# Modulation blocks summed beside projections, and narrow experts placed between wide ones

## What is computed

```python
# first block: layer 0 = even mixer, cross attention, dense swiglu (2816 hidden)
#              layer 1 = conformer convolution, cross attention, mixture of 8 experts (3584 hidden, top 2)
h = h + even_mixer(rmsnorm(h), ...);      h = h + cross_attn(rmsnorm(h), mem, ...)
h = h + swiglu(rmsnorm(h), w_gu, w_down)
h = h + conformer_conv(rmsnorm(h), ...);  h = h + cross_attn(rmsnorm(h), mem, ...)
h = h + moe_swiglu(rmsnorm(h), router, w_gu, w_down)
# second block: its layers are modulated by a vector c
cs = silu(c)
for l in range(2):
    mod = cs @ ada_w[l] + ada_b[l]        # 1024 x 6144 weights per layer
    sh1, sc1, g1, sh2, sc2, g2 = split(mod, 6)
    x = x + g1 * mixer_l(rms_norm(x, norm1_g[l]) * (1 + sc1) + sh1)
    x = x + g2 * hier_moe(rms_norm(x, norm2_g[l]) * (1 + sc2) + sh2, ...)   # 16 experts, 256 hidden
```

## Time and profile before

| | us |
|---|---|
| median of 3 runs | 2881.32 |
| lowest and highest | 2875.06, 2892.28 |
| the profiled execution, whole | 2874.71 |
| its span | 2872.9 |
| first mixture, first gather to last scatter | 985.5 |
| second block, first mixture, norm to norm | 225.9 |
| second block, second mixture, norm to norm | 212.6 |
| PE busy in the span | 2539.0 (88%) |
| DVE, ACT busy in the span | 794.5 (28%), 410.5 (14%) |

### The profile page before, as it was taken

One profiled execution on the slowest core, in us unless ns is written; L12 is line 12 of the kernel. 1 busy time (PEld: TensorE's weight loads), 2 busy tenths in 40 slices (PEclk: granted clock), 3 DMA queues, 4 the chain that ended last, 5 costly groups with the idle time before them and its releaser, 6 DMA issues. The chain is left out here.

```text
span 2872.9 us, 35384 instructions
## 1 busy us (share of the span) xinstructions
PE 2539.0 (88%) x15219; PEld 1502.3 (52%) x15219; DVE 794.5 (28%) x1806; ACT 410.5 (14%) x926; POOL 53.7 (2%) x67
## 2 busy tenths in 40 slices
PE   2889899998989999999997878689689977998997
PEld 2776788785773333333333323265554466656543
DVE  1211221288221122221212000124434413373122
ACT  1102000001121111011110000113211101352111
POOL 0000000070000000000000000000000000000000
PEclk9999999998989999999999999898879988697899
DMA  8333255642009999999999999932139962301481
GB/s 268 117 109 126 73 191 205 209 143 74 1 31 392 393 385 385 379 373 393 371 393 393 393 394 393 391 108 88 53 120 371 374 122 80 117 1 63 159 300 56
DMA packets 328586, 645.33 MB, mean 225 GB/s; under 512 B 12875, under 2 KB 98017, under 8 KB 328417
## 3 DMA queue, kind: packets, MB, share of 16 engines
q1 hardware_dynamic: 318608, 636.51, 61.4%
q10 hardware_dynamic: 9809, 6.41, 0.8%
HBM read 641.84 MB, written 1.05 MB: 224 GB/s over the span
## 5 line engine op out<-in xcount | busy, mean ns | idle before, releaser
L1330 PE MATMUL bank<-ring,xn 128*32 128x512 f32 x4896 | 564.3, 596 | 7.9 <-DMA ring<-od_moe_gu 6.2
L1142 PE MATMUL bank<-xn,ring 128*128 128x256 f32 x2048 | 462.9, 390 | 54.2 <-DVE xn L2878 17.7
L1142 PEld LDWEIGHTS bank<-xn,ring 128*128 128x128 f32 x2048 | 401.1, 196 | 116.6 <-issue 41.1
L1330 PEld LDWEIGHTS bank<-ring,xn 128*32 128x32 f32 x4896 | 157.1, 110 | 362.3 <-issue 349.0
L1395 PE MATMUL bank<-ring,att 128*32 128x512 f32 x2448 | 276.7, 593 | 1.3 <-ACT att L1961 1.3
L1295 PE MATMUL bank<-ring,xn 128*64 128x512 f32 x336 | 170.8, 658 | 64.9 <-issue 64.9
L2406 DVE TENSOR_TENSOR sq<-att,bank 32x512 f32<-32x512 f32 x70 | 48.0, 686 | 507.8 <-ACT att L1972 342.4
L1297 PE MATMUL bank<-ring,xn 128*64 128x512 f32 x336 | 171.2, 659 | 0.0
L1395 PEld LDWEIGHTS bank<-ring,att 128*32 128x32 f32 x2448 | 78.6, 110 | 171.9 <-issue 170.8
L1249 PE MATMUL bank<-xn,ring 128*128 128x256 f32 x704 | 153.6, 380 | 0.0
L1249 PEld LDWEIGHTS bank<-xn,ring 128*128 128x128 f32 x704 | 134.6, 191 | 18.7 <-issue 0.3
(11 more groups left out here) (265 smaller groups left out, 2324.0 us busy)
## 6 DMA issues: line engine op xcount, KB each, us to landing
ring<-od_moe_gu SPq DMA_DIRECT2D x112, 2048.0 KB, 17.3
ring<-od_moe_down SPq DMA_DIRECT2D x56, 2048.0 KB, 18.0
ring<-ada_w SPq DMA_DIRECT2D x24, 2048.0 KB, 15.1
ring<-moe_w_gate SPq DMA_DIRECT2D x32, 1024.0 KB, 9.2
ring<-moe_w_up SPq DMA_DIRECT2D x32, 1024.0 KB, 8.4
ring<-moe_w_down SPq DMA_DIRECT2D x16, 2048.0 KB, 13.8
ring<-ev_w_in SPq DMA_DIRECT2D x10, 2048.0 KB, 19.8
ring<-ev_ffn_gu SPq DMA_DIRECT2D x10, 2048.0 KB, 12.8
```

Of the source, the lines that this page charges most:

```text
L1142: mm = nc.tensor.matmul(ps[:, c * T:(c + 1) * T], kblk(b)[:, k, u * T + c * P:u * T + (c + 1) * P], x[:, k, :], start=k == 0, stop=k == KD ...
L1330: return nc.tensor.matmul(PSB[f.b][j * QP:(j + 1) * QP, :], src[:, k, at:at + QP], kblk(b)[:, k, :], start=k == 0, stop=k == KD - 1)
```

## The change

Three things. First, `linear` and `token_linear` take a function `beside`, and a turn of the modulation work stands beside a unit of a projection: its block in the ring behind the projection's block, its DVE sum in DVE's queue at that unit, and the PE sum of the turn before behind the unit. 3 blocks go beside the output projection of the even mixer, 9 beside keys, values and queries of the first cross attention, 5 stay in the dense stage, 4 go beside the queries of the second cross attention and 3 beside its output. That is all 24. The calls in the mixtures stay, but find nothing left. Outside the dense stage the partial sums lie in `att` in place of `sq`. Second, the scales that combine `mod` with the norms' gains are made before the norm of the first mixture, and no longer inside later stages. Third, the experts of the first mixture run in the order `TURNS` of the sorted loads: widths 96, 96, 64, 96, 64, 96, 96, 64. `st.i` is now the turn and `st.rank` the place in the sort.

```diff
+TURNS = [0, 1, 5, 2, 6, 3, 4, 7]
...
+        def ada_acc(a):
+
+            home = sq.rearrange("p k t -> p (k t)") if a.in_sq else att
+            return home[:, a.i % 2 * WBLK:(a.i % 2 + 1) * WBLK]
...
+        def ada_block(in_sq=True):
...
+            if ada_made[0] == 2 * ADA_BLOCKS:
+                return None
+            a = Stage()
+            a.i, a.in_sq = ada_made[0], in_sq
+            a.block = block(col_load(A["ada_w_2"][a.i // ADA_BLOCKS], a.i % ADA_BLOCKS * WBLK))
...
+            a.block.release = (ada_ready, a.n + 1)
+            ada_made[0] += 1
+            return a
...
+        def ada_turns(n):
+
+            left = [n]
+
+            def beside():
+                x = Stage()
+                made = left[0] > 0
+                left[0] -= made
+                ada_turn(x, ada_block(False) if made else None)
+                return x
+            return beside
+
+        def linear(W, c0, n, done, beside=None):
...
+            st.units, st.beside = [], []
             st.done = counted(done)
             for at in range(c0, c0 + n, WBLK):
                 b = block(col_load(W, at))
                 for u in range(2):
                     st.units.append((b, u, fill_turn((done, count(done, 1) + 1))))
+                    st.beside.append(beside() if beside is not None else None)
...
-        ev_out = linear(A["ev_w_out"][0], 0, D, h_ready)
+        ev_out = linear(A["ev_w_out"][0], 0, D, h_ready, ada_turns(3))
...
-            st.k = linear(A["xa_wkv"][l], 0, D, proj_ready)
-            st.v = token_linear(A["xa_wkv"][l], D, D, proj_ready)
+            st.k = linear(A["xa_wkv"][l], 0, D, proj_ready, beside)
+            st.v = token_linear(A["xa_wkv"][l], D, D, proj_ready, beside)
...
-            st.kv = memory_kv(l) if kv is None else kv
-            st.q = linear(A["xa_wq"][l], 0, D, proj_ready)
+            st.kv = memory_kv(l, beside) if kv is None else kv
+            st.q = linear(A["xa_wq"][l], 0, D, proj_ready, beside)
...
-            st.out = linear(A["xa_wo"][l], 0, D, h_ready)
+            st.out = linear(A["xa_wo"][l], 0, D, h_ready, beside_out)
...
-        cross0 = cross(0, ev_out.end, None)
+        cross0 = cross(0, ev_out.end, None, ada_turns(9))
...
-        cross1 = cross(1, pw2.end, kv1)
+        cross1 = cross(1, pw2.end, kv1, ada_turns(4), ada_turns(3))
...
-        for i, cap in enumerate(CAPS):
+        for n, i in enumerate(TURNS):
+            cap = CAPS[i]
...
-            st.i, st.width, st.gather, st.blocks = i, cap, gather_fills, (first_block, len(blocks))
+            st.i, st.rank, st.width, st.gather, st.blocks = n, i, cap, gather_fills, (first_block, len(blocks))
...
-                expert = sp.value_load(order[0:1, st.i:st.i + 1], min_val=0, max_val=E1 - 1)
+                expert = sp.value_load(order[0:1, st.rank:st.rank + 1], min_val=0, max_val=E1 - 1)
...
+            def sums_beside(st, i):
+                if st.beside[i] is not None:
+                    ada_sums(st.beside[i].ada)
+
             def pe_linear(st, x, ready):
                 for i, (b, u, f) in enumerate(st.units):
                     if u == 0:
                         landed(b)
                     unit(b, u, f, x, ready if i == 0 else None)
+                    sums_beside(st, i)
...
-                for b, c, f in st.units:
+                for i, (b, c, f) in enumerate(st.units):
                     if c == 0:
                         landed(b)
                     token_unit(b, c, f, x)
+                    sums_beside(st, i)
...
+            def steps_beside(st):
+                for x in st.beside:
+                    if x is not None:
+                        ada_step(x)
+
             def add_units(st):
 
                 for i, (b, u, f) in enumerate(st.units):
+                    if st.beside[i] is not None:
+                        ada_step(st.beside[i])
                     hp = h[:, 2 * i:2 * i + 2, :]
                     nc.vector.tensor_tensor(hp, full(f).rearrange("p (c t) -> p c t", c=2), hp, ALU.add)\
...
                     norm_memory(st.l)
+                    steps_beside(st.kv.k)
+                    steps_beside(st.kv.v)
+                steps_beside(st.q)
                 dve_attention(st.att)
                 add_units(st.out)
...
-                if l == 0:
-                    ada_scales(1)
...
+            dve.wait_ge(scalar_step, 1)
             add_units(ev_out)
             dve_cross(cross0, True)
             normalise(norm_ffn, vec("ev_norm_ffn"))
-            dve.wait_ge(scalar_step, 1)
...
+            ada_scales(0)
+            ada_scales(1)
             normalise(norm_moe, vec("od_norm_moe"))
...
-                    weigh_slots(st.i, P, "pairs").then_inc(scatter_ready, 1)
+                    weigh_slots(st.rank, P, "pairs").then_inc(scatter_ready, 1)
...
-                    take_slots(st.i + 1, CAPS[st.i + 1]).then_inc(gather_ready, 1)
+                    after_it = moe1[st.i + 1]
+                    take_slots(after_it.rank, after_it.width).then_inc(gather_ready, 1)
...
-            ada_scales(0)
```

More of the change, by code:

```diff
@@ L461, in row_load, with ada_turn @@
             return lambda b: (rblk(b)[:, to // P:(to + n) // P, :], src)
-        def linear(W, c0, n, done):
+        ADA_BLOCKS = 6 * D // WBLK
+        ada_made, ada_left = [0], []
+        def ada_block(in_sq=True):
[4 more added lines that the diff above has]
+            a.block = block(col_load(A["ada_w_2"][a.i // ADA_BLOCKS], a.i % ADA_BLOCKS * WBLK))
+            a.n = count(ada_ready, 1)
+            a.block.release = (ada_ready, a.n + 1)
+            ada_made[0] += 1
+            return a
+        def ada_turn(x, a):
+            x.ada, x.ada_in = list(ada_left), [a] if a else []
+            for given in x.ada:
+                given.fill = fill_turn()
+            ada_left[:] = x.ada_in
+        def ada_turns(n):
[8 more added lines that the diff above has]
+        def linear(W, c0, n, done, beside=None):
             st = Stage()
-            st.units = []
+            st.units, st.beside = [], []
             st.done = counted(done)
@@ L476, in linear, with token_linear @@
             return st
-        def token_linear(W, c0, n, done):
+        def token_linear(W, c0, n, done, beside=None):
             st = Stage()
-            st.units = []
+            st.units, st.beside = [], []
             st.done = counted(done)
@@ L502, in stacked_blocks_kernel @@
         chunks = []
[L503 to L523, removed]
         def ffn_steps(n_hidden, gate_up, down, ada_at=(), after_first=None):
@@ L674, in attention, with memory_kv @@
             return st
-        def memory_kv(l):
+        def memory_kv(l, beside=None):
             st = Stage()
@@ L679, in memory_kv, with cross @@
             st.memn = count(memn_ready, KD)
-            st.k = linear(A["xa_wkv"][l], 0, D, proj_ready)
-            st.v = token_linear(A["xa_wkv"][l], D, D, proj_ready)
+            st.k = linear(A["xa_wkv"][l], 0, D, proj_ready, beside)
+            st.v = token_linear(A["xa_wkv"][l], D, D, proj_ready, beside)
             return st
-        def cross(l, h_at, kv):
+        def cross(l, h_at, kv, beside, beside_out=None):
             st = Stage()
@@ L730, in stacked_blocks_kernel @@
             b.release = (bank_full[fs[1].b], fs[1].n)
-        pw1.sg = counted(sg_ready) - KD
+        pw1.sg, pw1.beside = counted(sg_ready) - KD, [None] * KD
         kv1 = memory_kv(1)
@@ L738, in stacked_blocks_kernel @@
         pw2 = linear(A["od_pw2_w"][0], 0, D, h_ready)
-        cross1 = cross(1, pw2.end, kv1)
+        cross1 = cross(1, pw2.end, kv1, ada_turns(4), ada_turns(3))
+        assert ada_made[0] == 2 * ADA_BLOCKS and not ada_left
         norm_moe = norm(cross1.out.end)
@@ L788, in stacked_blocks_kernel @@
                 st.before = prev.steps[-1].used
-            gather_fills = four_fills(gathered) if i + 1 < E1 else None
+            gather_fills = four_fills(gathered) if n + 1 < E1 else None
             moe1.append(st)
@@ L1465, in ada_sums @@
                     for j in range(WBLK // P):
-                        mm = nc.tensor.matmul(ps[:, j:j + 1], ada_acc(a.i)[:, j * P:(j + 1) * P], ones[:, 0:1],
+                        mm = nc.tensor.matmul(ps[:, j:j + 1], ada_acc(a)[:, j * P:(j + 1) * P], ones[:, 0:1],
                                               start=True, stop=True)
@@ L2466, in ada_sum @@
                     dve.wait_ge(slot_landed[a.block.slot], a.block.landed)
-                    w, y = kblk(a.block), ada_acc(a.i)
+                    w, y = kblk(a.block), ada_acc(a)
                     chain(nc.vector.tensor_scalar(y, w[:, 0, :], cs[:, 0:1], None, ALU.mult))
@@ L2827, in next_slots @@
                 if st.paired:
-                    weigh_slots(st.i, P, "pairs").then_inc(scatter_ready, 1)
+                    weigh_slots(st.rank, P, "pairs").then_inc(scatter_ready, 1)
                 else:
                     for to, which in zip(scatter_more, ("three0", "three1", "pairs")):
```

(5 more changed lines are left out.)

2 lines of the change are left out of this document (removed).

## The result

| | before | after |
|---|---|---|
| median, us | 2883.04 | 2861.81 |
| lowest and highest, 14 runs each | 2875.06, 2898.47 | 2856.27, 2879.16 |
| the profiled execution, whole | 2874.71 | 2872.88 |
| its span | 2872.9 | 2871.1 |

The ratio is 0.9926, with a 95% interval of 0.9902 to 0.9950: the change makes the kernel faster by 21 us, between 14 and 28 by the interval. The forecast was 46 us less; 2861.8 lies in its range, near the upper end. The profiled execution of after, though, is only 1.8 us shorter than that of before. So there are two questions: why the stages gave less than forecast, and where the profiled execution lost what they gave.

What follows compares the result with a forecast made beforehand. In the first mixture PE bounds wide experts and the weight stream narrow ones. Gains of 55.9 (first mixture) and 13.3 (second mixtures) less 22.8 (projections) make 46 us: 2881.3 - 46 = 2835 us, range 2810 to 2866.

Steps and rivals of the forecast that it cites:

- The lead of the narrow experts: First mixture: weights loaded ahead during wide experts shorten the narrow ones to 102, 102 and 111.2 us.
- The price of seven modulation blocks: Second block's first mixture: without them it matches its twin, 212.62 us in place of 225.90, 13.3 us gained.
- The wide experts: First mixture: PE sets the pace; without modulation sums they take 118, 125.3, 122.9, 122.9 and 125.3 us.
- the count of landings: Narrow expert behind a wide one: block arrivals counted slot by slot, up 6 landing at 89 us, 102 in all.
- Rival (a): First mixture: the ring gives no usable lead, narrow experts stay at 111.9, 111.9 and 121.7 us; 2865 us, chance 0.12.
- (b): First mixture: the lead is worth more and the mixture falls to the stream's time, 905 us; 2810 us, chance 0.08.
- The lower bound of the prediction: Second block's first mixture: PE's own sums for seven modulation blocks, 7 x 0.98 = 6.9 us gained at least.
- What the projections pay: Mixer's output and both attentions: the nineteen modulation blocks moved there cost 22.8 us.
- my two bounds: Projections: PE's sums for one modulation block cost between 0.81 and 0.98 us; 0.98 was taken.
- Rival (c): Projections: DVE's step does not fit beside a unit, each of 19 blocks costs 6.4 us more; 2957 us, chance 0.04.
- The late softmax: Second attention: DVE starts on the scores behind the fourth modulation block's sums, 4.6 us later.
- Rival (d): First mixture: the weight stream sags to 357 GB/s and the mixture gains nothing; 2891 us, chance 0.01.

Runs made afterwards that it cites:

- c2: The changed kernel with a weight ring of 6 slots in place of 7; 2908.85 us, ratio 1.0087.
- c1: The kernel before with the new order of the experts and nothing else; 2878.81 us, ratio 0.997.
- b3: The changed kernel with one modulation block moved from the second attention's queries to the first attention; 2866.6 us, ratio 0.9907.
- a3: The kernel before with sixteen dummy products put ahead of the last layer's compression; 2893.64 us, ratio 1.0005.
- a4: The changed kernel with the experts of the first mixture back in their old order; 2879.77 us, ratio 0.9945.
- b1: The kernel before with the operands of the compression's products exchanged; 2874.69 us, ratio 0.9949.
- b2: The changed kernel with the operands of the compression's products exchanged; 2844.96 us, ratio 0.9849.
- a1: The changed kernel run and profiled once more, nothing edited; 2862.19 us, ratio 0.9893.
- a2: The changed kernel with sixteen dummy products put ahead of the last layer's compression; 2861.55 us, ratio 0.9889.
- b4: The changed kernel with the compression's operands exchanged and one modulation block moved from the second attention's queries to the first; 2838.75 us, ratio 0.9834.

## Why the prediction was right or wrong

Three terms failed. The lead of the narrow experts was counted too large (102, 102 and 111.2 us; measured 108.5, 109.6 and 114.4). The price of seven modulation blocks in the second block's first mixture was set at 13.3 us and measured 7.0. And the clock of the last layer's compression was put at nothing: no term, only the 6.6 us between one execution and the median. Two smaller misses went the other way.

**The wide experts: right, and a little better.** Forecast 118, 125.3, 122.9, 122.9 and 125.3 us; measured 115.7, 125.0, 121.4, 121.4 and 125.0, together 5.9 us less. A wide expert behind a narrow one is 3.6 us shorter and not the 2.4 that I read from the earlier trace rows. The shorter scatter (3.3 us at 1247.74 in place of 5.4) is 2.1 of it; the rest is the last down product of the expert before, which also falls behind the gather (from start to next start 3.6 us for a narrow one, 5.2 for a wide one). The first expert lost all of its waiting but 1.2 us.

**The narrow experts: the mechanism right, the size wrong.** Forecast 102, 102 and 111.2; measured 108.5, 109.6 and 114.4, together 17.2 more. The step that failed is the count of landings. It put gate 3 into the slot of down 0 at 30.5 and landed up 3 at 41 and up 4 at 57. The rows have gate 3 issued at 32.6, step 3 begin at 46.1 and step 4 at 63.5, 6.5 late. From step 4 to the next gather it is 45 us, as counted (57 to 102); all of the miss is ahead of it.

The first 2.1 us are a wrong reading of the earlier trace rows. The count gave the narrow expert a scatter of 3.0 us ("the scatter to 19.4"), but the one that stands in it belongs to the expert before, a wide one, and takes 5.4: from 1140.91 to step 1 at 1146.29, and as much in before (1517.42 to 1522.86). I had used that rule for the wide experts and not for the narrow ones.

The other 4.4 us are the stream. The five blocks from gate 3 to up 4 take 31.0 us from issue to use where I allowed 5 x 5.32 = 26.6, a figure read from a stream that never pauses. Here it had stopped, and it moved only 35 GB/s in the first 1.95 us behind the issue. In the 29.0 us behind them it moved 393 GB/s, 11.4 MB, where five blocks are 10.5: part of the next block had come in before up 4 was whole. So the rows put about 2 us on the restart and about 2 on blocks that overlap; no run isolates either. That the lead in the ring is the source of the gain is shown by c2 and c1. Rival (a) is out, since the narrow experts behind a wide one did become shorter; so is (b).

**The first mixture** gave 44.6 us of the 55.9: 5.9 better and 17.2 worse.

**The second block's first mixture: wrong.** I took the whole difference of 13.3 us between it and its twin as the price of the modulation blocks. It gave 5.6 from norm to norm and 7.0 up to the next projection. Timeline of PE at its end in after, and the end of the twin in after:

```profile
2271.63 2.90 PE L1199 MATMUL bank<-sq,ones 128*128 128x256 f32 x6 [7.20 <-issue]
2278.23 4.11 PE L1199 MATMUL bank<-sq,ones 128*128 128x256 f32 x10 [3.71 <-issue]
...
2851.52 3.69 PE L1199 MATMUL bank<-sq,ones 128*128 128x256 f32 x16 [0.18 <-issue]
```

An idle time of 10.9 us at the norm belongs to the place and not to the blocks: it is there with them (5.12 and 5.58 us in before) and without, and the twin has 0.18. The 7.2 us of it that fall inside the window are nearly all of the 7.7 by which the stage still exceeds its twin. What fills them stays open: the squares that PE sums there were ready in `sq` at 2266.0, and the bracket names no engine. The lower bound of the prediction, 6.9 us for PE's own part, was close to the truth. Two stages that run the same code are not twins where their surroundings differ.

**What the projections pay: right.** Forecast 22.8 us, measured 18.7. A row of each kind in after:

```profile
153.96 0.95 PE L1490 MATMUL bank<-ones,att 128*128 128x1 f32 x8
154.77 7.15 PE L1160 MATMUL bank<-xn,ring 128*128 128x256 f32 x32
```

Units start 7.8 us apart, without a wait of PE for DVE; a sum pushes the next unit by 0.81 us, the lower of my two bounds (19 x 0.17 = 3.2 us of the difference). Rival (c) is out. The late softmax was counted as 4.6 us and measured by b3 as 4.1; its second price, the fallen clock, was not counted: of the 7.5 us, 4.1 are the wait and 0.8 the fourth block's sum, and 2.6 are left for it. Against before it costs less, since before runs part of this attention at half clock too: from the first transpose to the output projection it is 12.2 us in before, 13.0 in after and 10.5 in b3.

**The sum up to the last layer** was therefore 33 us and not 46.

**The clock: a term that was missing.** I made the sum against one execution, added the 6.6 us between it and the median, and so took for granted that the changed kernel would draw the same clock. The compression's clock differs between executions of one program. Nine traces have the products of 60 columns: the first piece ran at full clock in six of them (not in after, a3 and a4), the second in one alone, that of before. So the execution that the sum was made against was the exception, with full clock in both pieces, and that of after had neither. The medians are medians over such draws: they differ by 21 us in the first comparison and by 34 in the second (2896.5 and 2862.2). With the draw removed (b1, b2) it is 29.7. So 13 us of the miss are in the stages. The 12 between 33 and 21 I put down to the clock; that is argued from the pairs and not measured by itself, since single traces cannot give the share of each draw in a median. A hint stood in the times shown: three runs from 2875 to 2892, 17 us apart.

On the clock the Trainium skill (page "TensorE: Matmul & The Clock Gate", section "Why this matters for your kernels") tells to avoid drops by leaving no idle gap between bursts of products. The trace agrees in the attention of after, where the products behind a wait run at half clock (3.62 us for 1.89). It does not in the compression: the second piece of a1 ran at 0.53 with PE busy for 26.15 of 26.15 us, behind one at 0.98. That every load of the mixture would be held to about 358 GB/s (page "DMA: Bandwidth & Descriptors", section "Bandwidth") is not what the rows of after show: 393 and 394 GB/s over 116 and 121 us. The same section has more for a core that streams alone and keeps that figure for two at once, and with that the rows agree: one core runs here. Rival (d) is out.

## What to carry to other kernels

Work that is moved out of a stage bound by a stream gives back its own time and also the lead that the stream then builds, but only as much of it as the buffers hold, and only if stages with a need for it stand behind ones with time to spare: the two parts were worth 8.2 us more together than singly. Count a stream that has run empty by its own rows, not by the rate of one that never pauses. Ask of each piece of work in a stage whose it is: here the scatter and the last down product belong to the stage before. Do not price a removed step by the difference of two stages with different neighbours. Before a few per cent are judged, look for a stage whose time differs between executions of one kernel, and take that difference out of both kernels; here exchanging the operands of one product was worth 21 us in the kernel before and 17 in the changed one.

## What the runs showed of the hardware

PE's granted clock fell to half inside a stretch of products of 60 columns with weights of 128 x 128, with PE busy all the time, in some executions and not in others of the same program (14.4 to 15.2 us a piece against 25.9 to 27.6). The second of the two pieces was at half clock in eight of nine traces, the first in three. A first piece at full clock, and in a2 sixteen products of 512 columns ahead of it, did not hold the second one up (26.7 us in a2). The same sums with 256 columns streamed over weights of 60 columns ran at 0.94 in b2 and took 13.8 to 15.5 us in all three traces of b1, b2 and b4. With 60 columns a weight load is about as long as the product: the weight loader was busy for 30.26 of 31.17 us in before's compression and for 18.54 of 32.90 in b2's. Whether that, or the number of columns, is what the clock answers to, no run here tells apart.

A weight stream that had stopped moved 35 GB/s in the first 1.95 us behind the next issue, and 393 GB/s over the 29.0 us behind them (after, first narrow expert).
